# The second block's rotary embeddings: the swapped half read by VectorE from another 32-partition quadrant, in place of a permutation product on TensorE

## The chip, the cores and the metric

The kernel runs on one core of a Trainium2 chip. The metric is the device time of one execution in microseconds (us); it was measured three times before the change, and one further execution was profiled.

## What is computed

Two transformer blocks in fp32, batch 1, 256 tokens, width 2048. The first has latent and differential attention and a convolutional GEGLU feed-forward part. The second has sparse attention with compressed, selected and windowed keys (the "A" half, heads of 128) and banded attention with a sink (the "B" half, heads of 64). The change concerns the rotary embedding of the second block alone:

```python
def _rope(x):
    ang = jnp.arange(S)[:, None] * inv[None, :]
    x1, x2 = xf[..., : d // 2], xf[..., d // 2:]
    return jnp.concatenate([x1 * cos - x2 * sin, x2 * cos + x1 * sin], axis=-1)

# in second_block, after proj = h @ w_in
qa = _rope(heads of 128);  kca, ksa, kwa = _rope(heads of 128)
qb = _rope(heads of 64);   kb = _rope(heads of 64)
```

## The kernel before

Activations lie transposed: features on the 128 partitions, the 256 tokens along the free axis, one tile of 128 features by 256 tokens after another. So a head of 128 is one tile, and its halves are partitions 0 to 63 and 64 to 127. Two heads of 64 share a tile, and each has its halves in two neighbouring groups of 32 partitions.

Every fp32 weight is streamed once from HBM in halves of 128 x 1024 elements (512 KB) through a ring of eight slots, `raw`. For each half ScalarE makes a rounded copy `w_hi` (`hi`, L1138), then VectorE the remainder `w_lo` = `raw` - `w_hi` (`lo`, L1568). TensorE then takes three products for each 128 x 128 tile (L609 to L611). `w_hi` and `w_lo` are rings of four halves: half h+4 can be split once TensorE has finished half h. When `lo` of a half has run, its slot in `raw` is loaded again.

The stretch that matters is the second block's input projection, a loop over j = 0 to 46, one output tile ("unit") for each j: 16 weight tiles, two halves, 48 matmuls. Each engine has its own instruction stream with the same loop, and semaphores tie them together. In step j:

- TensorE does unit j, then for j = 31 to 38 a `compress` unit (two more halves of weights, 24 products in all, L992 to L994), then in some steps a rotation's product (`rotate`, L714), and from j = 13 on the attention work of one head.
- ScalarE splits the halves (`ahead`), and does exponentials and copies.
- VectorE does `ahead(u, 0)`, which is `lo` of the half four ahead of unit j's first; takes unit j out of PSUM into `proj2` (L2117, waits for the end of unit j); from j = 13 the softmax pieces (`first_half`); `ahead(u, 1)`; for j = 31 to 38 two more `lo`; and after all that, in twelve of the steps, a rotation (`rope2`).

A rotation takes one tile (j = 2) or two (j = 3, 5, 7, 9, 20, 24, 26, 33, 35, 37, 39). TensorE multiplies the tiles, in fp32, by a 128 x 128 matrix of 0, 1 and -1 (`swap32` for heads of 64, `swap64` for heads of 128) into PSUM; this gives the other half of each pair with its sign. VectorE then multiplies that by the sine (L1702), the tiles in place by the cosine (L1704), and adds (L1706):

```python
V.tensor_tensor(part, ps[:, bank, 0:n * S]..., sin..., ALU.mult).then_inc(rot_used, 1)
V.tensor_tensor(tiles, tiles, cos..., ALU.mult).then_inc(rope_cos, 1)
dve.wait_ge(rope_cos, at + 1)
V.tensor_tensor(tiles, tiles, part, ALU.add).then_inc(roped, 1)
dve.wait_ge(roped, at + 1)
```

`part` is the last quarter of `dk_second`. The tiles that step j rotates were taken out in steps up to j - 1, so TensorE's wait ahead of its product is for the evacuation of unit j - 1.

Of the kernel before, what the change touches and what calls it, by code (L numbers as in the profile page):

```python
# [23 lines left out]
P = 128  # L24
S = 256
# [245 lines left out]
def build_program(nc, A):  # L271
    from contextlib import ExitStack
    ctx = ExitStack()
    with ctx:
# [3 lines left out]
        def sem(name):  # L278
            return ctx.enter_context(nc.semaphore(name))
# [108 lines left out]
            sem("sub_sq"), sem("sub_mean"), sem("sub_root"), sem("sub_raw"), sem("sub_hi"), sem("sub_lo"))  # L388
        sub_ms, sub_inv, sub_wide = sem("sub_ms"), sem("sub_inv"), sem("sub_wide")
        lat_norm, lat_hi, lat_lo = sem("lat_norm"), sem("lat_hi"), sem("lat_lo")  # L390
        rope_cos = sem("rope_cos")
        conv_center, gelu_done, prod_done, g_hi_done, g_lo_done = (
            sem("conv_center"), sem("gelu_done"), sem("prod_done"), sem("g_hi_done"), sem("g_lo_done"))
        y_zero = sem("y_zero")
# [208 lines left out]
        def _(pe):  # L603
# [105 lines left out]
            def rotate(at, bank, src, tile, swap, n, used=0):  # L709

                if used:
                    pe.wait_ge(rot_used, used)
                for k in range(n):
                    last = nc.tensor.matmul(ps[:, bank, k * S:k * S + S], con(swap), src[:, tile + k, :],  # L714
                                            start=True, stop=True)
                last.then_inc(rot_ready, 1)
# [329 lines left out]
            for j in range(N_IN2):  # L1046
                tiles = range(KT) if j < N_IN2 - 1 else [*range(HEADS, KT), *range(HEADS)]
                if j >= 2:
                    unit(U2["in", j], tiles, h_hi, h_lo, middle=(lambda: compress_scores(0)) if j == 42 else None)
                before = EVAC_COUNT[U2["in", j]] - 1  # L1050
                if j == CMP_AFTER:
                    pe.wait_ge(tok_copied, 15)
                if CMP_AFTER <= j < CMP_AFTER + 8:
                    compress(j - CMP_AFTER)
                if j == 2:
                    pe.wait_ge(unit_evac, before)
                    rotate(3, 5, proj2, KB, "swap32", 1)
                elif j == 4:
                    pe.wait_ge(roped, 4)
                    nc.tensor.matmul(ps[:, OUT, 0:S], con("swap64"), proj2[:, KB, :], start=True, stop=True  # L1060
                                     ).then_inc(swap_ready, 1)
                elif j in (3, 5, 7, 9):
                    pe.wait_ge(unit_evac, before)
                    at = 4 + (j - 3) // 2
                    rotate(at, 5, proj2, QB + j - 3, "swap32", 2, at)
                elif j == 10:
                    pe.wait_ge(unit_evac, before)
                    pe.wait_ge(rot_used, 8)
                    to_tokens(12, proj2, [VB], 1)
                elif j == 20:  # L1070
                    pe.wait_ge(unit_evac, before)
                    pe.wait_ge(tok_copied, 13)
                    rotate(8, 5, proj2, KCA, "swap64", 2)
                elif j == 24:
                    pe.wait_ge(unit_evac, before)
                    rotate(9, 5, proj2, KSA, "swap64", 2, 9)
                elif j == 26:
                    pe.wait_ge(unit_evac, before)
                    rotate(10, 5, proj2, KWA, "swap64", 2, 10)
                elif j == 28:  # L1080
                    pe.wait_ge(unit_evac, before)
                    pe.wait_ge(rot_used, 11)
                    to_tokens(13, proj2, [VSA])
                elif j == 30:
                    pe.wait_ge(unit_evac, before)
                    pe.wait_ge(tok_copied, 14)
                    to_tokens(14, proj2, [VWA])
                elif j in (33, 35, 37, 39):
                    pe.wait_ge(unit_evac, before)
                    at = 11 + (j - 33) // 2  # L1090
                    rotate(at, SCORE + (at - 11) % 2, proj2, QA + j - 33, "swap64", 2, at - 1)
                elif j == 40:
                    pe.wait_ge(unit_evac, before)
                    pe.wait_ge(rot_used, 14)
                    to_tokens(15, proj2, [GA], 1)
                if j == 13:
                    pe.wait_ge(roped, 8)
                    pe.wait_ge(tok_copied, 13)
                    pe.wait_ge(swap_copied, 2)
                    pe.wait_ge(pad_ready, HEADS + 3)  # L1100
                elif j == A_STEP:
                    pe.wait_ge(roped, 15)
                    pe.wait_ge(tok_copied, 16)
                if j == 36:
                    compress_rows(0)
                elif j == 40:
                    compress_rows(1)
                elif j == 41:
                    compress_kv()
                elif j == 42:  # L1110
                    compress_scores(1)
                if B_STEP <= j < B_STEP + 19:
                    step(b_maps, j - B_STEP)
                if j == N_IN2 - 1:
                    pe.wait_ge(cmp_T_copied, 2)
                if j >= A_STEP:
                    step(a_maps, j - A_STEP)
                if j in (44, 45):
                    compress_turn(j - 44)
# [441 lines left out]
        def _(dve):  # L1561
# [134 lines left out]
            def rope(at, bank, scratch, src, tile, n, cos, sin, out=None):  # L1696

                dve.wait_ge(rot_ready, at + 1)
                part = scratch[:, 0:n * S].rearrange("p (a b) -> p a b", a=n)
                wide = [P, n, S]  # L1700
                tiles = src[:, tile:tile + n, :]
                V.tensor_tensor(part, ps[:, bank, 0:n * S].rearrange("p (a b) -> p a b", a=n),  # L1702
                                sin.unsqueeze(1).broadcast_to(wide), ALU.mult).then_inc(rot_used, 1)
                V.tensor_tensor(tiles, tiles, cos.unsqueeze(1).broadcast_to(wide), ALU.mult).then_inc(rope_cos, 1)  # L1704
                dve.wait_ge(rope_cos, at + 1)
                V.tensor_tensor(tiles if out is None else out, tiles, part, ALU.add).then_inc(roped, 1)  # L1706
                dve.wait_ge(roped, at + 1)
# [388 lines left out]
                if a < len(some):  # L2096
                    maxima(some[a])

            def rope2(at, bank, tile, d, n=2):
                rope(at, bank, rope_part.rearrange("p a b -> p (a b)"), proj2, tile, n, con(f"cos{d}"), con(f"sin{d}"))  # L2100

            def b_low():

# [6 lines left out]
            for j in range(N_IN2):  # L2110
                u = U2["in", j]
                if j == N_IN2 - 1:
                    b_low()
                if j:
                    ahead(u, 0)
                dve.wait_ge(gemm_step, unit_step(u))
                V.tensor_tensor(proj2[:, IN2_TILES[j], :], ps[:, BANK[u], 0:S], rstd[:, NORM["x2"] % 2, :], ALU.mult  # L2117
                                ).then_inc(unit_evac, 1)
                if B_STEP <= j < B_STEP + 17:
                    first_half(b_maps, j - B_STEP)  # L2120
                if j >= A_STEP:
                    first_half(a_maps, j - A_STEP)
                if j:
                    ahead(u, 1)
                if CMP_AFTER <= j < CMP_AFTER + 8:
                    for part in range(2):
                        ahead(U2["cmp", j - CMP_AFTER], part)
                if j == 2:
                    rope2(3, 5, KB, 64, 1)
                elif j in (3, 5, 7, 9):  # L2130
                    rope2(4 + (j - 3) // 2, 5, QB + j - 3, 64)
                elif j == 20:
                    rope2(8, 5, KCA, 128)
                elif j == 22:
                    dve.wait_ge(roped, 9)
                    compress_input(0, KCA, "k_pos", None)
                elif j == 24:
                    rope2(9, 5, KSA, 128)
                    split_blocks(0)
                elif j == 25:  # L2140
                    compress_input(1, VCA, "v_pos", U2["in", 21])
                elif j == 26:
                    rope2(10, 5, KWA, 128)
                elif j == 27:
                    split_blocks(1)
                elif j in (33, 35, 37, 39):
                    at = 11 + (j - 33) // 2
                    rope2(at, SCORE + (at - 11) % 2, QA + j - 33, 128)
                elif j == 42:
                    compress_shift()  # L2150
                elif j == 43:
                    compress_normalise()
                a = j - B_STEP
                if 3 <= a < len(b_maps) + 3 and b_maps[a - 3]["last"]:
                    take_b(b_maps[a - 3])
# [205 lines left out]
```

## Time and profile before

| what | value |
|---|---|
| median of 3 runs | 1762.83 us (1761.37 to 1764.17) |
| the profiled execution's own time | 1761.64 us |
| its span, first to last instruction | 1759.8 us |
| TensorE (PE) busy | 1696.8 us, 96% of the span |
| VectorE (DVE) busy | 1251.7 us, 71% |
| ScalarE (ACT) busy | 892.1 us, 51% |
| mean granted TensorE clock | 0.985 |
| DMA | 377.10 MB, mean 214 GB/s |
| load of one half of weights, issue to landing | 3.8 us |

The busy times of the engines overlap. Matmuls are pipelined in the rows: a product of the main stream shows 0.28 us, but they start every 0.12 us, so what one costs is read from the distance of starts. The input projection of the second block takes about 1285 to 1605 us of the span. A time such as 1517.36 is in us from the first instruction.

### The profile page before, as it was taken

How to read it: one execution, taken by the hardware profiler on the slowest of the kernel's cores; microseconds unless marked ns; L12 is line 12 of the kernel's file. 1: busy time of each engine (PE TensorE's matmuls, PEld its weight loads, DVE VectorE, ACT ScalarE, POOL GpSimd, SP SyncE). 2: the span in 40 equal slices, each digit the busy share in tenths (PEclk: the TensorE clock that was granted, in tenths of full speed). 3: DMA queues.
4: the chain of work that ended last, by engine and by line, in shares of the span. 5: the costliest groups of instructions: out<-in, count | busy, mean ns of one | idle time of the engine just before them, and what ended most of it. 6: DMA issues, size and time to landing. Idle time of an engine off the chain costs nothing.

```text
span 1759.8 us, 33243 instructions
## 1 busy us (share of the span) xinstructions
PE 1696.8 (96%) x13841; PEld 1654.6 (94%) x13841; DVE 1251.7 (71%) x1877; ACT 892.1 (51%) x1445; POOL 19.7 (1%) x31
## 2 busy tenths in 40 slices
PE   2899999999999999999999999999999999999997
PEld 2799999999999999999999999999899999999997
DVE  6888899898787667667667656656865576665655
ACT  8545445555565445445445435535734544446554
POOL 0000010000000000000000000000000000000000
PEclk7899999999999999999999999999999999999999
DMA  9899787688647666667667666565355444764341
GB/s 366 337 359 375 253 296 287 243 296 328 259 159 231 209 205 227 214 204 229 209 193 232 217 187 183 180 189 183 109 169 168 144 133 132 225 209 130 111 128 63
DMA packets 89285, 377.10 MB, mean 214 GB/s; under 512 B 10032, under 2 KB 10416, under 8 KB 76592
## 3 DMA queue, kind: packets, MB, share of 16 engines
q1 hardware_dynamic: 89136, 374.98, 62.7%
q8 instruction: 110, 1.80, 0.4%
q14 instruction: 39, 0.32, 0.1%
HBM read 372.84 MB, written 2.10 MB: 213 GB/s over the span
## 4 chain that ended last, share of the span: by engine, by line
PE 89%; DVE 5%; DMA 3%; issue 1%; ACT 1%; DVEq 0%; SPq 0%; ACTq 0%
PE ps L609 26%; PE ps L610 25%; PE ps L611 25%; PE ps L730 4%; DMA raw<-in_ada 3%; DVE raw L1577 2%; PE ps L764 1%; PE ps L749 1%; PE ps L772 1%; DVE w_lo L1568 1%; PE ps L714 1%; PE ps L992 0%; PE ps L994 0%; PE ps L993 0%; PE ps L638 0%
## 5 line engine op out<-in xcount | busy, mean ns | idle before, releaser
L609 PE MATMUL ps<-h_hi,w_hi 128*128 128x256 f32 x3248 | 938.4, 289 | 8.3 <-DVE h_lo L1641 5.2
L610 PE MATMUL ps<-h_lo,w_hi 128*128 128x256 f32 x3248 | 920.4, 283 | 0.0
L611 PE MATMUL ps<-h_hi,w_lo 128*128 128x256 f32 x3248 | 920.2, 283 | 0.0
L1568 DVE TENSOR_TENSOR w_lo<-raw,w_hi 128x1024 fp32r<-128x1024 f32 x510 | 622.7, 1223 | 262.7 <-ACT w_hi L1138 261.7
L1138 ACT ACTIVATE w_hi<-raw 128x1024 fp32r<-128x1024 f32 x510 | 538.6, 1058 | 511.5 <-PE ps L611 466.5
L609 PEld LDWEIGHTS ps<-h_hi,w_hi 128*128 128x128 f32 x3248 | 624.2, 192 | 16.7 <-issue 11.5
L610 PEld LDWEIGHTS ps<-h_lo,w_hi 128*128 128x128 f32 x3248 | 624.7, 192 | 1.2
L611 PEld LDWEIGHTS ps<-h_hi,w_lo 128*128 128x128 f32 x3248 | 624.4, 192 | 0.0
L1577 DVE SCALAR_TENSOR_TENSOR raw<-raw,c_wide 128x2048 f32<-128x2048 f32 x96 | 219.3, 2287 | 18.3 <-DMA raw<-in_ada 17.4
L609 PE MATMUL ps<-g_hi,w_hi 128*128 128x256 f32 x704 | 199.3, 283 | 0.6 <-DVE conv L1975 0.6
L610 PE MATMUL ps<-g_lo,w_hi 128*128 128x256 f32 x704 | 199.2, 283 | 0.0
L611 PE MATMUL ps<-g_hi,w_lo 128*128 128x256 f32 x704 | 199.2, 283 | 0.0
L609 PEld LDWEIGHTS ps<-g_hi,w_hi 128*128 128x128 f32 x704 | 135.2, 192 | 0.8 <-DVE conv L1975 0.8
L611 PEld LDWEIGHTS ps<-g_hi,w_lo 128*128 128x128 f32 x704 | 135.2, 192 | 0.0
L610 PEld LDWEIGHTS ps<-g_lo,w_hi 128*128 128x128 f32 x704 | 135.2, 192 | 0.0
L1390 ACT ACTIVATE conv<-ps,params 128x256 f32<-128x256 f32 x88 | 49.8, 565 | 148.5 <-PE ps L611 148.5
L1972 DVE SCALAR_TENSOR_TENSOR conv<-ps,params,conv 128x255 f32<-128x255 f32 x88 | 42.5, 483 | 79.4 <-ACT conv L1390 79.4
L1206 ACT ACTIVATE probs<-ps,stats 128x128 f32<-128x128 f32 (+1 forms) x112 | 48.8, 440 | 50.7 <-DVE stats L1720 43.9
L2003 DVE TENSOR_TENSOR y<-ps,y 128x256 f32<-128x256 f32 x96 | 40.4, 423 | 44.4 <-PE ps L611 44.4
L1716 DVE TENSOR_REDUCE stats<-ps 128x1 f32<-128x128 f32 (+1 forms) x112 | 37.7, 377 | 19.8 <-PE ps L733 19.6
L1975 DVE SCALAR_TENSOR_TENSOR conv<-ps,params,conv 128x255 f32<-128x255 f32 x88 | 42.5, 483 | 3.1
L1221 ACT ACTIVATE probsT<-ps 128x384 f32<-128x384 f32 (+1 forms) x56 | 29.9, 534 | 18.3 <-PE ps L749 16.9
(237 smaller groups left out, 1208.6 us busy)
## 6 DMA issues: line engine op xcount, KB each, us to landing
raw<-in_weights SPq DMA_DIRECT2D x510, 512.0 KB, 3.8
raw<-in_ada SPq DMA_DIRECT2D x96, 1024.0 KB, 6.0
x<-in_x SPq DMA_DIRECT2D x1, 2048.0 KB, 12.7
out_y<-x SPq DMA_DIRECT2D x3, 512.0 KB, 2.9
c_wide<-in_c_wide SPq DMA_DIRECT2D x1, 1024.0 KB, 5.4
consts<-in_consts SPq DMA_DIRECT2D x1, 798.0 KB, 8.9
out_y<-x SPq DMA_DIRECT2D x2, 256.0 KB, 2.6
params<-in_params SPq DMA_DIRECT2D x1, 504.0 KB, 7.4
```

What stands on the lines that cost most here:

```text
L609: nc.tensor.matmul(out, wh, hi[:, k, :], start=start, stop=False)
L610: nc.tensor.matmul(out, wh, lo[:, k, :], start=False, stop=False)
L611: last = nc.tensor.matmul(out, wl, hi[:, k, :], start=False, stop=stop)
L730: last = nc.tensor.matmul(out, q(qt), k(qt, w), start=a == 0, stop=a == n_terms - 1 and not masked)
L1138: nc.scalar.activation(w_hi[:, h % W_SLOTS, :], raw[:, raw_slot("w", h), :], ACT.Copy).then_inc(hi_split, 1)
L1206: last = nc.scalar.activation(probs[:, s, off:off + w], ps[:, SCORE + i % 2, off:off + w], ACT.Exp, bias=stats[:, s, 2 + qt:3 + qt], scale ...
L1390: nc.scalar.activation(conv[:, j, :], ps[:, BANK[u], 0:S], ACT.Identity, bias=params[:, col + b:col + b + 1], scale=params[:, col + w1:col ...
L1568: V.tensor_tensor(w_lo[:, h % W_SLOTS, :], raw[:, raw_slot("w", h), :], w_hi[:, h % W_SLOTS, :].bitcast(F32), ALU.subtract).then_inc(lo_dv ...
L1577: V.scalar_tensor_tensor(out=part, in0=part, scalar=1.0, in1=c_wide[:, :, :], op0=ALU.mult, op1=ALU.mult, accum_out=mod_raw[:, v, t:t + 1] ...
L1972: V.scalar_tensor_tensor(out=conv[:, j, 1:S], in0=ps[:, BANK[u], 0:S - 1], scalar=params[:, w0:w0 + 1], in1=conv[:, j, 1:S], op0=ALU.mult, ...
L1975: V.scalar_tensor_tensor(out=conv[:, j, 0:S - 1], in0=ps[:, BANK[u], 1:S], scalar=params[:, w2:w2 + 1], in1=conv[:, j, 0:S - 1], op0=ALU.m ...
L2003: V.tensor_tensor(y[:, f, :], ps[:, BANK[u], 0:S], y[:, f, :], ALU.add).then_inc(unit_evac, 1)
```

## The change

On TensorE the twelve `rotate` calls of the second block go, with their waits (23 fp32 products, each of a 128 x 128 matrix with 256 columns). Two waits that stood in front of them or guarded the PSUM banks move to the next user or go. On VectorE the single sine product, which read PSUM, becomes four `scalar_tensor_tensor` instructions of 32 partitions each: each reads a group of 32 partitions of the tiles and the same group of the sine table, multiplies by 1 or -1, and writes another group of `part`. For heads of 64 groups 0 and 1, and 2 and 3, change places; for heads of 128 groups 0 and 2, and 1 and 3. The cosine product now waits for all four. The first block's rotations and the one `swap64` product at j = 4 stay on TensorE.

```diff
-                if j == 2:
-                    pe.wait_ge(unit_evac, before)
-                    rotate(3, 5, proj2, KB, "swap32", 1)
-                elif j == 4:
+                if j == 4:
...
-                elif j in (3, 5, 7, 9):
-                    pe.wait_ge(unit_evac, before)
-                    at = 4 + (j - 3) // 2
-                    rotate(at, 5, proj2, QB + j - 3, "swap32", 2, at)
                 elif j == 10:
                     pe.wait_ge(unit_evac, before)
-                    pe.wait_ge(rot_used, 8)
                     to_tokens(12, proj2, [VB], 1)
-                elif j == 20:
+                elif j == 28:
                     pe.wait_ge(unit_evac, before)
                     pe.wait_ge(tok_copied, 13)
-                    rotate(8, 5, proj2, KCA, "swap64", 2)
...
-                elif j in (33, 35, 37, 39):
-                    pe.wait_ge(unit_evac, before)
-                    at = 11 + (j - 33) // 2
-                    rotate(at, SCORE + (at - 11) % 2, proj2, QA + j - 33, "swap64", 2, at - 1)
...
-            def rope2(at, bank, tile, d, n=2):
-                rope(at, bank, rope_part.rearrange("p a b -> p (a b)"), proj2, tile, n, con(f"cos{d}"), con(f"sin{d}"))
+            def rope2(at, u, tile, d, n=2):
+
+                part, shape = rope_part[:, 0:n, :], [32, n, S]
+                tiles = proj2[:, tile:tile + n, :]
+                dve.wait_ge(unit_evac, EVAC_COUNT[u] - 1)
+                for q in range(4):
+                    away = (1 if d == 64 else 2)
+                    src = q ^ away
+                    rows = slice(32 * src, 32 * src + 32)
+                    V.scalar_tensor_tensor(out=part[32 * q:32 * q + 32], in0=tiles[rows], scalar=-1.0 if q < src else 1.0,
+                                           in1=con(f"sin{d}")[rows].unsqueeze(1).broadcast_to(shape),
+                                           op0=ALU.mult, op1=ALU.mult).then_inc(rope_sine, 1)
+                dve.wait_ge(rope_sine, 4 * (at - 2))
+                V.tensor_tensor(tiles, tiles, con(f"cos{d}").unsqueeze(1).broadcast_to([P, n, S]), ALU.mult
+                                ).then_inc(rope_cos, 1)
+                dve.wait_ge(rope_cos, at + 1)
+                V.tensor_tensor(tiles, tiles, part, ALU.add).then_inc(roped, 1)
+                dve.wait_ge(roped, at + 1)
```

What this does to VectorE's stream is seen in step 33, the first rotation of the query heads of 128 (`proj` is `proj2`, `consts` holds the tables). Before, with what each instruction waits for:

```order
L2117 TENSOR_TENSOR proj<-ps,rstd 128x256 [waits gemm_step]
L1568 TENSOR_TENSOR w_lo<-raw,w_hi 128x1024 [waits hi_split] x3
L1702 TENSOR_TENSOR dk_second<-ps,consts 128x512 [waits rot_ready]
L1704 TENSOR_TENSOR proj<-proj,consts 128x512
L1706 TENSOR_TENSOR proj<-proj,dk_second 128x512 [waits rope_cos]
L1568 TENSOR_TENSOR w_lo<-raw,w_hi 128x1024 [waits hi_split,roped]
```

And now:

```order
L2110 TENSOR_TENSOR proj<-ps,rstd 128x256 [waits gemm_step]
L1545 TENSOR_TENSOR w_lo<-raw,w_hi 128x1024 [waits hi_split] x3
L2085 SCALAR_TENSOR_TENSOR dk_second<-proj,consts 32x512 [waits unit_evac]
L2085 SCALAR_TENSOR_TENSOR dk_second<-proj,consts 32x512 x3
L2089 TENSOR_TENSOR proj<-proj,consts 128x512 [waits rope_sine]
L2092 TENSOR_TENSOR proj<-proj,dk_second 128x512 [waits rope_cos]
L1545 TENSOR_TENSOR w_lo<-raw,w_hi 128x1024 [waits hi_split,roped]
```

Three instructions more stand between the `lo` ahead of the rotation and the `lo` behind it, and the cosine product has a wait that it had not.

On TensorE, at the end of step 33 (the last product of `compress`, the rotation, the first product of unit 34), before:

```order
L994 MATMUL ps<-w_hi,cmp_xl 30x256
L714 MATMUL ps<-proj,consts 128x256 [waits rot_used,unit_evac]
L714 MATMUL ps<-proj,consts 128x256
L609 MATMUL ps<-h_hi,w_hi 128x256 [waits lo_dve,unit_evac]
L610 MATMUL ps<-h_lo,w_hi 128x256
```

And now:

```order
L994 MATMUL ps<-w_hi,cmp_xl 30x256
L609 MATMUL ps<-h_hi,w_hi 128x256 [waits lo_dve,unit_evac]
L610 MATMUL ps<-h_lo,w_hi 128x256
```

The two fp32 products and their wait are gone; unit 34's first product still waits for its `lo` and for its PSUM bank.

## Rows read from the trace of the kernel before

**Rows 1.** Busy time by stretch: us, then PE, PEld, DVE, ACT, POOL, clock, DMA.

```profile
1285.00:1605.00 320.00, 320.00 (x2568) 305.65 (x2567) 200.02 (x324) 150.68 (x224) 1.01 (x3) 1.00 0.54 168
1500.00:1580.00 80.00, 80.00 (x657) 77.32 (x656) 52.65 (x56) 37.15 (x40) 0.00 (x0) 1.00 0.72 225
1605.00:1755.00 150.00, 144.89 (x1132) 135.16 (x1131) 92.36 (x218) 80.33 (x165) 0.00 (x0) 0.99 0.30 96
```

**Rows 2.** Who waited for whom, 1285 to 1605: us, times, longest.

```profile
ACT w_hi L1138 <- PE ps L611: 153.4, 80, 3.6
DVE w_lo L1568 <- ACT w_hi L1138: 94.6, 77, 4.0
DVE proj L2117 <- PE ps L611: 20.0, 38, 2.3
PEld ps L609 <- issue: 3.0, 17, 0.2
```

**Rows 3.** The rotations' products, 1285 to 1600, grouped by line and form.

```profile
L714 PE MATMUL ps<-proj,consts 128*128 128x256 f32 x46 | 11.9, 379 | 0.0
```

**Rows 4.** TensorE in order of time at steps 2 and 33: start, us.

```profile
1287.29 0.28 PE L611 MATMUL ps<-h_hi,w_lo 128*128 128x256 f32 x1
1287.41 0.59 PE L714 MATMUL ps<-proj,consts 128*128 128x256 f32 x2
...
1287.96 0.28 PE L610 MATMUL ps<-h_lo,w_hi 128*128 128x256 f32 x1
...
1517.24 0.28 PE L994 MATMUL ps<-w_hi,cmp_xl 128*30 128x256 f32 x1
1517.36 1.02 PE L714 MATMUL ps<-proj,consts 128*128 128x256 f32 x4
...
1518.34 0.28 PE L610 MATMUL ps<-h_lo,w_hi 128*128 128x256 f32 x1
```

**Rows 5.** The chain that ended last: first and last of eleven such lines.

```profile
1293.75 0.86 PE ps L714 x4
...
1569.29 0.86 PE ps L714 x4
```

**Rows 6.** VectorE in order of time at step 33, with idle time before.

```profile
1518.71 1.23 DVE L1568 TENSOR_TENSOR w_lo<-raw,w_hi 128x1024 fp32r<-128x1024 f32 x1 [0.15 <-ACT w_hi L1138]
1519.85 0.68 DVE L1702 TENSOR_TENSOR dk_second<-ps,consts 128x512 f32<-128x512 f32 x1
1520.45 0.68 DVE L1704 TENSOR_TENSOR proj<-proj,consts 128x512 f32<-128x512 f32 x1
1521.17 0.69 DVE L1706 TENSOR_TENSOR proj<-proj,dk_second 128x512 f32<-128x512 f32 x1
1522.52 1.23 DVE L1568 TENSOR_TENSOR w_lo<-raw,w_hi 128x1024 fp32r<-128x1024 f32 x1 [0.66 <-ACT w_hi L1138]
```

**Rows 7.** `scalar_tensor_tensor` forms of VectorE: count, us, mean ns, idle.

```profile
L1827 DVE SCALAR_TENSOR_TENSOR cs<-cs 128x256 f32<-128x256 f32 x3 | 1.3, 425 | 0.1
L1927 DVE SCALAR_TENSOR_TENSOR proj<-proj,lam,ps 128x512 f32<-128x512 f32 x4 | 2.7, 740 | 0.0
```

**Rows 8.** Line L1811, four copies of groups 0 to 3: durations, then in order of time.

```profile
L1811 DVE COPY delta<-delta_parts x4: 152/156/160, 9.5 to 10.0; 32x24 bf16<-32x24 bf16 x4
...
9.50 0.66 DVE L1811 COPY delta<-delta_parts 32x24 bf16<-32x24 bf16 x4
```

**Rows 9.** The ScalarE split ahead of that last `lo`, and the weight load that needs it.

```profile
1521.36 1.06 ACT L1138 ACTIVATE w_hi<-raw 128x1024 fp32r<-128x1024 f32 x1 [2.68 <-PE ps L611]
...
1526.66 0.19 PEld L609 LDWEIGHTS ps<-h_hi,w_hi 128*128 128x128 f32 x1
```

**Rows 10.** VectorE in order of time, steps 24 and 25.

```profile
1443.91 0.68 DVE L1702 TENSOR_TENSOR dk_second<-ps,consts 128x512 f32<-128x512 f32 x1
...
1445.96 1.16 DVE L2055 TENSOR_TENSOR cmp_xl<-dk_second,cmp_xh 128x960 fp32r<-128x960 f32 x1
1447.33 1.23 DVE L1568 TENSOR_TENSOR w_lo<-raw,w_hi 128x1024 fp32r<-128x1024 f32 x1 [0.22 <-ACT w_hi L1138]
1449.06 0.42 DVE L2117 TENSOR_TENSOR proj<-ps,rstd 128x256 f32<-128x256 f32 x1 [0.51 <-PE ps L611]
...
1457.02 0.42 DVE L2117 TENSOR_TENSOR proj<-ps,rstd 128x256 f32<-128x256 f32 x1 [0.50 <-PE ps L611]
```

**Rows 11.** TensorE's four transposed-row products at step 36, in the chain.

```profile
1544.83 0.56 PE ps L1002 x4
```

More of the change, by code:

```diff
@@ L390, in build_program @@
         lat_norm, lat_hi, lat_lo = sem("lat_norm"), sem("lat_hi"), sem("lat_lo")
-        rope_cos = sem("rope_cos")
+        rope_cos, rope_sine = sem("rope_cos"), sem("rope_sine")
         conv_center, gelu_done, prod_done, g_hi_done, g_lo_done = (
@@ L1061, in _ @@
                                      ).then_inc(swap_ready, 1)
-                elif j in (3, 5, 7, 9):
-                    pe.wait_ge(unit_evac, before)
-                    at = 4 + (j - 3) // 2
-                    rotate(at, 5, proj2, QB + j - 3, "swap32", 2, at)
                 elif j == 10:
                     pe.wait_ge(unit_evac, before)
-                    pe.wait_ge(rot_used, 8)
                     to_tokens(12, proj2, [VB], 1)
-                elif j == 20:
+                elif j == 28:
                     pe.wait_ge(unit_evac, before)
                     pe.wait_ge(tok_copied, 13)
-                    rotate(8, 5, proj2, KCA, "swap64", 2)
-                elif j == 24:
-                    pe.wait_ge(unit_evac, before)
[L1076 to L1082, printed above, removed]
                     to_tokens(13, proj2, [VSA])
@@ L1087, in _ @@
                     to_tokens(14, proj2, [VWA])
-                elif j in (33, 35, 37, 39):
-                    pe.wait_ge(unit_evac, before)
-                    at = 11 + (j - 33) // 2
-                    rotate(at, SCORE + (at - 11) % 2, proj2, QA + j - 33, "swap64", 2, at - 1)
                 elif j == 40:
                     pe.wait_ge(unit_evac, before)
-                    pe.wait_ge(rot_used, 14)
                     to_tokens(15, proj2, [GA], 1)
@@ L2128, in _ @@
                 if j == 2:
-                    rope2(3, 5, KB, 64, 1)
+                    rope2(3, u, KB, 64, 1)
                 elif j in (3, 5, 7, 9):
-                    rope2(4 + (j - 3) // 2, 5, QB + j - 3, 64)
+                    rope2(4 + (j - 3) // 2, u, QB + j - 3, 64)
                 elif j == 20:
-                    rope2(8, 5, KCA, 128)
+                    rope2(8, u, KCA, 128)
                 elif j == 22:
@@ L2137, in _ @@
                 elif j == 24:
-                    rope2(9, 5, KSA, 128)
+                    rope2(9, u, KSA, 128)
                     split_blocks(0)
@@ L2142, in _ @@
                 elif j == 26:
-                    rope2(10, 5, KWA, 128)
+                    rope2(10, u, KWA, 128)
                 elif j == 27:
@@ L2147, in _ @@
                     at = 11 + (j - 33) // 2
-                    rope2(at, SCORE + (at - 11) % 2, QA + j - 33, 128)
+                    rope2(at, u, QA + j - 33, 128)
                 elif j == 42:
```

## The prediction

> **What bounds the kernel now.** I read the busy time by stretch first. In the input projection of the second block TensorE is busy for 320.00 of 320.00 us, at the full granted clock of 1.00, which is the 2.4 GHz level; VectorE is busy for 200.02 and ScalarE for 150.68 us, and the DMA engines for 0.54 of it [rows 1]. After it, up to 1755 us, TensorE is still busy for 144.89 of 150 us. Next the list of waits for the same 320 us: the other two engines wait for TensorE (ScalarE 153.4 us before a split, VectorE 20.0 us before it takes out a unit, and 94.6 us for ScalarE, which itself waits for TensorE). The longest entry of the weight loads is "issue", 3.0 us over 17 times, and no line names a DMA [rows 2]. So this stretch is as long as TensorE's work, and everything behind it starts relative to TensorE. Work taken off TensorE comes off the end, as long as `w_lo` stays ahead of it.
>
> **What goes from TensorE.** The page counts 46 records of the rotation's product, two for each of 23 fp32 products [rows 3]. Their shown length (379 ns) overlaps, so I take the distance of starts. In step 2, one product: L611 starts at 1287.29, and without a rotation the next L610 would start two pitches of 0.12 us later, at 1287.53; it starts at 1287.96 [rows 4]. One product costs 0.43 us. In step 33, two products: L994 starts at 1517.24, the second product of the next unit would start at 1517.48, and starts at 1518.34 [rows 4]: 0.86 us. The chain that ended last names the two-product rotation eleven times with the same 0.86 us [rows 5]. Sum: 11 x 0.86 + 0.43 = 9.9 us, all on the path. The semaphore waits that go with them cost nothing: no idle time of TensorE stands before them [rows 2]. For the same reason the two waits that are kept and moved (steps 28 and 10) are taken at nothing; what they wait for was done a step before.
>
> **What comes to VectorE.** Now a rotation starts at 1519.85, the next two instructions at 1520.45 and 1521.17, and the last ends at 1521.86 [rows 6]. An instruction that waits for nothing starts 0.60 us after one of 512 elements; one that waits for its predecessor's semaphore, 0.72 us after it. The new four have 32 partitions and 512 elements each. No row here has that form, so I bound it. The time of a VectorE instruction goes by the elements of a partition: 512 take 0.683 and 1024 take 1.23 us [rows 6], which gives about 0.41 us at 256; the `scalar_tensor_tensor` of 256 elements with a constant took 0.425 us, one of 512 with a scalar from memory and PSUM took 0.740 [rows 7]. I take 0.695 for the new ones, between 0.68 and 0.74. Partitions bring no discount: four copies of 32 partitions with 24 elements took 0.152 to 0.160 us each [rows 8], and nothing in those rows looks like a quarter.
>
> Next the distance. Those four copies, each on another group of 32 partitions, took 0.66 us together, (0.66 - 0.156) / 3 = 0.168 us apart, so none began before the one in front had ended [rows 8]; the 0.60 us between instructions of 0.68 that stay on all partitions [rows 6] is an overlap. The new four change their group each time, so I take 0.71 us apart and 0.1 us lost before the first. The Trainium skill (VectorE: DVE Perf Modes, section "Two Vector instructions with no wait between them") gives this as a rule: an instruction whose input or output starts in another 32-partition quadrant than the last one's is held until all earlier ones have finished. By the rule the four stand a full duration apart, without it 0.60; the sum for the kernel is the same 9.9 us by either, if the margin below holds.
>
> A rotation of two tiles then runs: first of four at 1519.95, last at 1522.08, cosine at 1522.80, sum at 1523.52, and the `lo` behind it can start at 1524.24. Before, that `lo` could have started at 1521.90 for VectorE, and did at 1522.52, when ScalarE had finished its half. VectorE gets 2.3 us more in each of eleven steps and some 1.4 in step 2, about 27 us. It had 120 us idle in the stretch [rows 1], so its sum of work is covered; the question is how late one `lo` may be.
>
> **Where the cover is thinnest.** The tightest steps are those in which `compress` follows the next unit, since its halves are used up in 1.4 us each: 33, 35 and 37. The `lo` behind the rotation of step 33 is the first half of unit 35, which TensorE's weight load took up at 1526.66 [rows 9]. With the rotation's 0.86 us gone TensorE gets there at 1525.80. The `lo` now ends at 1524.24 + 1.23 = 1525.47, and with 0.1 us for the signal (a split that ended at 1522.42 let VectorE start at 1522.52, [rows 6, 9]) TensorE may go on at 1525.57: 0.23 us to spare, where before it had 2.8. With the four 0.60 us apart the margin is 0.66 us; with 0.75 us apart (the 0.740 row) it is 0.07. Step 37 has the same order of work. Step 35 has 0.56 us more, since four small products stand in TensorE's way to unit 37 [rows 11]. I cost all three at nothing. If the four are dearer, each 0.1 us more costs up to 0.4 us in each of them, once: behind it come four `lo` with room to catch up.
>
> Elsewhere the room is wide. In step 24, where the rotation is followed by a 1.16 us split of the compressed input [rows 10], VectorE gets to its next `lo` at about 1449.4 instead of 1447.33 and to the evacuation of unit 25 some 2.3 us late. That `lo` is for unit 27, wanted behind unit 26, which ends just before 1457.02 [rows 10]: over 5 us to spare. The softmax pieces behind it run a step ahead of the transposes that need them. In steps 3 to 9 and 39 there is no `compress` behind, and a `lo` has three halves of 2.9 us (24 products, 0.12 us apart). VectorE's lateness also delays loads, since `lo` frees the slot: by at most 2.4 us in a ring of eight halves, with DMA at 0.72 in the densest part [rows 1] and no wait for it [rows 2].
>
> **Sum.** 1761.64 (the profiled execution) - 9.9 + 0 = 1751.7 us. The median of the three runs is 1.2 us above that execution, so I say 1762.83 - 9.9 = 1752.9 us.
>
> **Rivals.**
> 1. *Part of it comes back as waits for `w_lo` in steps 33, 35 and 37.* For: the margin of 0.23 us rests on a price for which there is no row. With the four 1.0 us apart the loss is 4 x 0.29 - 0.23 = 0.93 us in steps 33 and 37 and 0.37 in step 35, together 2.2 us: 1755.1 us. Against: the nearest rows lie at 0.60 to 0.75.
> 2. *No change that can be told.* The four cost twice the nearest row, 1.42 us apart: 12 x 0.71 - 1.25 = 7.3 us lost in the three steps, 1760.2 us. For: reading one group and writing another in the same instruction is not in the trace (the copies of [rows 8] kept their group). Against: those copies show no such cost for a change of group from one to the next.
> 3. *Slower.* VectorE runs such an instruction at a quarter of the rate, about 2.8 us each. In the same three steps 12 x 2.13 - 1.25 = 24.3 us of waiting for `w_lo` against 9.9 saved: 1777.2 us. The point of no gain is 12 x (p - 0.71) - 1.25 = 9.9, p = 1.64 us apart; slower by 0.2% begins at 1.93 us, 2.7 times the nearest row. Nothing in the profile speaks for it but the absence of a row.
>
> On the second and third only a page has a statement: the Trainium skill (Vector Engine (DVE) Microarchitecture Reference, section 3.8) says that a 32-partition operation may write to any quadrant at no cost. No row here shows it.
>
> **How the numbers follow.** 0.2% of this kernel is 3.5 us, about what a measurement can tell from no change. The full saving I give 0.86, the partial one 0.08 (between 3.5 and 9 us saved), no change 0.03, slower 0.03. So faster has 0.94, same 0.03, slower 0.03. The three runs lay within 1.5 us of their median, which puts the full saving at 1751.4 to 1754.4; the range reaches a little below, for a fast set of runs, and above to 1756.5, to take in most of the first rival: 1750.5 to 1756.5.
>
> **What will show it.** In the changed profile the 46 records of the rotation's product are gone from this stretch, and VectorE's evacuations of units 33 and 34 stand 0.86 us closer than before. The four 32-partition instructions read 0.68 to 0.74 us, and their group of four 2.8 to 2.9 us. TensorE has no wait on `w_lo` in steps 33 to 39. A wait there of more than 0.1 us would show the margin too small; a wait of TensorE in steps 20 to 28 would show that I misread the room of the softmax pieces; and a total saving below 9 us without a wait on TensorE would mean that the 0.86 us was not all the products' own. The prediction goes wrong if the new form costs over 0.9 us, or if a cost of one instruction on TensorE hides in the pitch of the main stream.

## The result and the profile after

The changed kernel takes 1753.05 us (median of 4 runs, 1751.56 to 1754.85), against 1762.1 us (4 runs, 1761.04 to 1764.17) for the one before. The ratio is 0.9946, with a 95% interval of 0.9933 to 0.9959; that is 7 to 12 us less. 1752.9 us was forecast. The profiled execution has a span of 1749.7 us, 10.1 us under that of before, and the median lies 9.05 us under.

The busy times by stretch of the changed kernel, in the columns of [rows 1] (the first row is the input projection of the second block, 10 us shorter than before; the last is the work behind it):

```profile
1285.00:1595.00 310.00, 310.00 (x2521) 296.84 (x2520) 223.06 (x360) 150.21 (x225) 1.34 (x3) 1.00 0.55 174
1500.00:1570.00 70.00, 70.00 (x587) 67.97 (x586) 56.60 (x63) 35.20 (x38) 0.00 (x0) 1.00 0.70 229
1595.00:1745.00 150.00, 144.74 (x1131) 135.02 (x1129) 92.42 (x218) 80.24 (x165) 0.00 (x0) 0.99 0.31 96
```

TensorE is still busy without a gap, at the full clock; VectorE is busy for 23 us more in 10 us less time and fills 81% of the densest part, where it filled 66%. The work behind the stretch is as it was.

The list of waits of the changed kernel, 1285 to 1600 us:

```profile
ACT w_hi L1115 <- PE ps L611: 143.2, 80, 3.6
DVE w_lo L1545 <- ACT w_hi L1115: 66.4, 51, 4.0
DVE proj L2110 <- PE ps L611: 14.4, 25, 2.3
...
PEld ps L609 <- issue: 3.2, 18, 0.2
```

VectorE's own idle time has shrunk (94.6 to 66.4 us before `lo`, 20.0 to 14.4 before an evacuation, [rows 2]); TensorE's has not grown (the eighteenth entry of L609, 0.2 us, stands at 1597.44 in the stretch behind; with the window drawn out to 1611 the kernel before has 18 too).

Step 33, VectorE in order of time, which answers to [rows 6] (a merged row names how many instructions it holds):

```profile
1511.99 1.23 DVE L1545 TENSOR_TENSOR w_lo<-raw,w_hi 128x1024 fp32r<-128x1024 f32 x1 [0.16 <-ACT w_hi L1115]
1513.25 2.83 DVE L2085 SCALAR_TENSOR_TENSOR dk_second<-proj,consts 32x512 f32<-32x512 f32 x4
1516.11 0.69 DVE L2089 TENSOR_TENSOR proj<-proj,consts 128x512 f32<-128x512 f32 x1
1516.84 0.69 DVE L2092 TENSOR_TENSOR proj<-proj,dk_second 128x512 f32<-128x512 f32 x1
1517.56 1.22 DVE L1545 TENSOR_TENSOR w_lo<-raw,w_hi 128x1024 fp32r<-128x1024 f32 x1
```

And the weight load that waits for this last `lo`, as in [rows 9]:

```profile
1519.08 0.19 PEld L609 LDWEIGHTS ps<-h_hi,w_hi 128*128 128x128 f32 x1
```

From the start of the `lo` in front to the start of the `lo` behind it is 5.57 us, against 5.53 forecast. That `lo` ends at 1518.78; with 0.1 us for the signal 0.2 us are to spare.

### The profile page after: what moved, and what is told of

It reads as the page before. It is cut to its first block, busy times and chain, and to the rows that moved or that the text cites. A ratio compares the mean times of both kernels' runs of the same rounds, so it can differ in the third digit from the quotient of the medians.

```text
span 1749.7 us, 33174 instructions
## 1 busy us (share of the span) xinstructions
PE 1688.6 (97%) x13795; PEld 1646.9 (94%) x13795; DVE 1275.7 (73%) x1913; ACT 891.1 (51%) x1445; POOL 20.0 (1%) x31
## 4 chain that ended last, share of the span: by engine, by line
PE 88%; DVE 5%; DMA 4%; issue 1%; ACT 1%; SPq 0%; DVEq 0%; ACTq 0%
PE ps L609 26%; PE ps L610 25%; PE ps L611 25%; PE ps L730 4%; DMA raw<-in_ada 4%; DVE raw L1554 2%; PE ps L764 2%; PE ps L749 1%; PE ps L772 1%; DVE w_lo L1545 1%; PE ps L992 0%; PE ps L993 0%; PE ps L994 0%; PE ps L638 0%; PE ps L652 0%
## 5 line engine op out<-in xcount | busy, mean ns | idle before, releaser
L609 PE MATMUL ps<-h_hi,w_hi 128*128 128x256 f32 x3248 | 936.5, 288 | 6.7 <-DVE h_lo L1618 4.4
L611 PE MATMUL ps<-h_hi,w_lo 128*128 128x256 f32 x3248 | 919.9, 283 | 0.0
L609 PEld LDWEIGHTS ps<-h_hi,w_hi 128*128 128x128 f32 x3248 | 624.0, 192 | 15.3 <-issue 9.8
L611 PEld LDWEIGHTS ps<-h_hi,w_lo 128*128 128x128 f32 x3248 | 624.1, 192 | 0.0
L609 PE MATMUL ps<-g_hi,w_hi 128*128 128x256 f32 x704 | 199.3, 283 | 0.6 <-DVE conv L1952 0.6
L611 PE MATMUL ps<-g_hi,w_lo 128*128 128x256 f32 x704 | 199.2, 283 | 0.0
L609 PEld LDWEIGHTS ps<-g_hi,w_hi 128*128 128x128 f32 x704 | 135.2, 192 | 0.8 <-DVE conv L1952 0.8
L611 PEld LDWEIGHTS ps<-g_hi,w_lo 128*128 128x128 f32 x704 | 135.2, 192 | 0.0
## 6 DMA issues: line engine op xcount, KB each, us to landing
x<-in_x SPq DMA_DIRECT2D x1, 2048.0 KB, 12.7
```

Of the source, the lines that this page charges most:

```text
L609: nc.tensor.matmul(out, wh, hi[:, k, :], start=start, stop=False)
L611: last = nc.tensor.matmul(out, wl, hi[:, k, :], start=False, stop=stop)
```

## The experiments

The first four ran on one chip, the next four on a second and key_copies on a third, with the kernel before beside them at 1761.7, 1761.1 and 1761.8 us. A median of four runs is good to about 1 us, so effects under that are read in the traces.

**products_kept: is it the products?**

```diff
+                if j in ROTATIONS:
+                    n, bank = ROTATIONS[j]
+                    for k in range(n):
+                        nc.tensor.matmul(ps[:, bank, k * S:k * S + S], con("swap64"), con("cos128"),
+                                         start=True, stop=True)
```

> The changed kernel, but TensorE still makes its 23 fp32 products in the same steps, of the permutation matrix with the cosine table, into the same PSUM banks; nobody reads them and VectorE does not wait for them. Theory A (the saving is what the products cost on TensorE, 0.43 us one and 0.86 us two): all of it goes back, 9.9 us above the changed kernel, 1763 us. Theory C (the saving came from VectorE no longer waiting for TensorE, or from PSUM banks that come free earlier): the time stays near 1753 us.

1763.1 us, ratio to the kernel before 1.0009 (1.0000 to 1.0019). The whole saving is gone with the new VectorE code in place, so the saving is what the products cost. The waits and the PSUM banks that came free are worth nothing that can be measured; the median lies 1.4 us above that of the kernel before, at the edge of what the runs tell. The products that were kept look in the trace as the old ones did ([rows 3]):

```profile
L1080 PE MATMUL ps<-consts 128*128 128x256 f32 x46 | 11.9, 378 | 0.0
```

**no_swap_at_all: did VectorE's new work take a part?**

```diff
-                for q in range(4):
...
+                V.tensor_tensor(part, tiles, con(f"sin{d}").unsqueeze(1).broadcast_to([P, n, S]), ALU.mult
+                                ).then_inc(rope_sine, 4)
```

> The changed kernel with one sine product of 128 partitions in place of the four of 32; it multiplies each half by its own sine and not by the other half's, so the rotation is not computed; VectorE's work is as before the change, and TensorE has no products. Theory A: VectorE's 27 us lie under TensorE, so the time is that of the changed kernel, 1753 us within 1 us. Theory B (part of the saving was lost again to VectorE's new work): faster than the changed kernel by what was lost, 1 us or more.

1751.45 us, ratio 0.9947 (0.9933 to 0.9962), against 0.9946 for the change; its span is 1749.6 us against 1749.7. VectorE's added work costs nothing that can be measured, and the waits of the weight loads in this stretch are the same in both traces.

**one_more: how thin is the cover?**

```diff
-                for q in range(4):
+                for at_q, q in enumerate([0, 1, 2, 3, 0]):
...
+                    to = part if at_q < 4 else gated[:, 0:n, :]
```

> The changed kernel with a fifth 32-partition instruction in each rotation, into a buffer that nobody reads. It makes the rotation 0.71 us longer. In the changed kernel's trace the lo behind step 33's rotation ends at 1518.78 and the weight load that needs it starts at 1519.08; with 0.1 us for the signal 0.2 us are to spare. Theory A (thin margin): a wait of TensorE of 0.5 us in step 34 and another in step 38, none in step 36, where 0.56 us more stand in between, and none elsewhere: 1754 us. Theory B (the margin is wide): no wait and the changed kernel's time.

1751.87 us, ratio 0.9951 (0.9936 to 0.9965): the 1 us is below what the runs tell. The trace tells it. These are the two weight loads that find their `lo` late, with the idle time in front; in the changed kernel there is none at these places:

```profile
1518.94 0.19 PEld L609 LDWEIGHTS ps<-h_hi,w_hi 128*128 128x128 f32 x1 [0.55 <-issue]
1554.34 0.19 PEld L609 LDWEIGHTS ps<-h_hi,w_hi 128*128 128x128 f32 x1 [0.55 <-issue]
```

Behind the rotations of steps 33 and 37, and not behind that of step 35, as expected. 0.71 us more gave 0.55 us of waiting: the margin was about 0.16 us.

**twice: where does VectorE begin to bound?**

```diff
+                for at_q, q in enumerate([0, 1, 2, 3, 0, 1, 2, 3]):
```

> The changed kernel with each of the four 32-partition instructions made twice, the second time into a buffer that nobody reads: 2.84 us more in each rotation of two tiles. Theory A (thin margin): waits of TensorE of 2.6 us after the rotations of steps 33 and 37 and of 2.1 us after that of step 35, 7.3 us together, 1760.4 us; no wait after the other rotations, though VectorE has the same work more there. Theory B (wide margin): the changed kernel's time. If VectorE were the bound by its sum of work, 12 times 2.8 us would come on top: 1787 us.

1767.2 us, ratio 1.0036 (1.0023 to 1.0049): slower than before the change, and twice the loss that was expected. The weight loads that waited, by place:

```profile
1306.03 0.19 PEld L609 LDWEIGHTS ps<-h_hi,w_hi 128*128 128x128 f32 x1 [0.80 <-issue]
1318.53 0.19 PEld L609 LDWEIGHTS ps<-h_hi,w_hi 128*128 128x128 f32 x1 [0.94 <-issue]
1331.04 0.19 PEld L609 LDWEIGHTS ps<-h_hi,w_hi 128*128 128x128 f32 x1 [0.95 <-issue]
1343.54 0.19 PEld L609 LDWEIGHTS ps<-h_hi,w_hi 128*128 128x128 f32 x1 [0.71 <-issue]
...
1457.38 0.19 PEld L764 LDWEIGHTS ps<-probsT,proj 128*64 128x64 f32 x2 [1.23 <-issue]
1474.55 0.19 PEld L764 LDWEIGHTS ps<-probsT,proj 128*64 128x64 f32 x2 [1.00 <-issue]
...
1527.72 0.19 PEld L609 LDWEIGHTS ps<-h_hi,w_hi 128*128 128x128 f32 x1 [2.69 <-issue]
1547.45 0.19 PEld L609 LDWEIGHTS ps<-h_hi,w_hi 128*128 128x128 f32 x1 [1.99 <-issue]
1567.23 0.29 PEld L609 LDWEIGHTS ps<-h_hi,w_hi 128*128 128x128 f32 x1 [2.70 <-issue]
```

The last three are the 7.3 us that were expected (2.69 + 1.99 + 2.70 = 7.4). Two groups were not. In steps 3 to 9 the first four rows stand 12.5 us apart: a rotation comes every second step, and two steps of VectorE then hold four `lo`, two evacuations and a rotation of 7.2 us, more than TensorE's two units of 5.75 us. Each `lo` there had room, but the sum over two steps had not; that makes 3.4 us. Behind the rotations of steps 24 and 26 a product of the attention (L764) waited for a PSUM bank that VectorE empties at the end of its step (L1754), which makes 1.9 us beyond the usual 0.17. The waits sum to 12.7 us, where the profiled span is 15.2 us above that of the changed kernel. A part of the rest is the clock. The stretch with the last wait and the one behind it:

```profile
1565.00:1570.00 5.00, 2.74 (x13) 2.77 (x14) 4.93 (x7) 0.96 (x1) 0.00 (x0) 0.72 0.33 107
1570.00:1575.00 5.00, 5.00 (x41) 5.00 (x41) 2.31 (x3) 1.23 (x2) 0.00 (x0) 0.94 0.88 291
```

The granted clock fell to a mean of 0.72 and 0.94 and was back at 1.00 after that. Cut into single microseconds, it is 1.00 up to 1567, 0.50 (the 1.2 GHz level) from 1568 to 1570, when TensorE is busy again, and 1.00 from 1571. I estimate the loss at 5 x 0.28 + 5 x 0.06 = 1.7 us. The last 0.8 us are not traced.

**one_group and own_group: what sets the distance of the four?**

```diff
-                    src = q ^ away
+                    src = 0
+                    to = (part, gated[:, 0:n, :], proj2[:, ZA + 4:ZA + 4 + n, :], proj2[:, ZA + 6:ZA + 6 + n, :])[q]
...
+                    V.scalar_tensor_tensor(out=to[0:32], in0=tiles[rows], ...
```

That is one_group. In own_group the edit is `src = q` alone, with the output as in the change.

> The changed kernel, but all four 32-partition instructions read partitions 0 to 31 and write partitions 0 to 31 of four different buffers, so none changes its group; the rotation is not computed. If a change of group is what holds each of the four until the one in front has ended, they stand 0.60 us apart here (4 of them in 2.5 us) instead of 0.71 (2.8 us). If the distance comes with 32 partitions or with this operation, it stays 2.8 us. The total stays that of the changed kernel, 1753 us.

> The changed kernel, but each of the four reads and writes its own group of partitions (0, 1, 2, 3), so the group changes from one to the next but never between input and output; the rotation is not computed. If the change from one instruction to the next holds them, 2.8 us for the four; if it is the crossing within an instruction, 2.5 us. Duration of one 0.68 us in either case if crossing is free, less than that if crossing costs. Total 1753 us.

Step 33 of one_group:

```profile
1514.32 0.67 DVE L2086 SCALAR_TENSOR_TENSOR dk_second<-proj,consts 32x512 f32<-32x512 f32 x1
1514.92 0.67 DVE L2086 SCALAR_TENSOR_TENSOR gated<-proj,consts 32x512 f32<-32x512 f32 x1
1515.52 1.28 DVE L2086 SCALAR_TENSOR_TENSOR proj<-proj,consts 32x512 f32<-32x512 f32 x2
```

And of own_group:

```profile
1516.54 2.82 DVE L2085 SCALAR_TENSOR_TENSOR dk_second<-proj,consts 32x512 f32<-32x512 f32 x4
```

One group: 0.60 us apart, 2.48 us for the four. Own group, without any crossing: 2.82 us, as in the change with its crossing (2.83). So the 0.11 us comes with the change of group from one instruction to the next, and reading one group and writing another costs nothing. One_group also writes to four buffers where own_group writes to one. That this is not what lets its instructions overlap is seen in a row of the kernel before, four `scalar_tensor_tensor` of 0.740 us into one tile, all on the same partitions:

```profile
336.37 2.71 DVE L1927 SCALAR_TENSOR_TENSOR proj<-proj,lam,ps 128x512 f32<-128x512 f32 x4
```

They stand (2.71 - 0.740) / 3 = 0.66 us apart, less than one of them takes. As for crossing, the median duration is 0.682 us without and 0.684 us with it. The single times, 1753.3 and 1755.3 us, say nothing against the expectation of 1753.

**halves_of_64: fewer instructions.**

```diff
+                size = d // 2
+                for q in range(P // size):
+                    src = q ^ 1
...
+                    V.scalar_tensor_tensor(out=part[size * q:size * q + size], in0=tiles[rows], ...
```

> The changed kernel, with two instructions of 64 partitions in place of four of 32 for the heads of 128. The rotation of two tiles is 1.4 us shorter on VectorE in steps 20 to 39. Theory A: TensorE did not wait in those steps, so the time stays within 1 us of the changed kernel's, 1753 us, and the margin behind step 33's rotation grows from 0.2 to 1.6 us. Theory B (some of the saving is lost to VectorE's work): faster by 1 us or more. An instruction of 64 partitions takes 0.68 us like one of 32.

1753.19 us, ratio 0.9951 (0.9938 to 0.9965), and two instructions of 64 partitions take 1.40 us, half of 2.83:

```profile
1513.36 1.40 DVE L2085 SCALAR_TENSOR_TENSOR dk_second<-proj,consts 64x512 f32<-64x512 f32 x2
...
1516.24 1.22 DVE L1545 TENSOR_TENSOR w_lo<-raw,w_hi 128x1024 fp32r<-128x1024 f32 x1
```

1.4 us of VectorE's time in each of seven rotations is given back and the kernel is no faster: that time was not on the path. The `lo` of the second row ends at 1517.46 and the weight load that needs it starts at 1519.18, so the margin is 1.6 us, as expected.

**all_on_vector and key_copies: can the other products go too?**

```diff
-                    rotate(0, 5, proj1, KR, "swap32", 1)
...
-                    rotate(1, 5, uq, QR, "swap32", 2, 1)
...
-                    rotate(2, 5, uq, QR + 2, "swap32", 2, 2)
...
-                    nc.tensor.matmul(ps[:, OUT, 0:S], con("swap64"), proj2[:, KB, :], ...
+                    V.tensor_copy(proj2[0:64, KB + 1, :], proj2[64:128, KB, :]).then_inc(swap_copied, 1)
+                    V.tensor_copy(kb_second[64:128, 0, :], proj2[0:64, KB, :]).then_inc(swap_copied, 1)
```

all_on_vector has the whole of it, with four instructions of 32 partitions in the first block's `rope` as well; key_copies only the last three lines. Both stand on halves_of_64. With the product of the keys go the two copies by which ScalarE took it out of PSUM.

> The kernel before it, with the first block's three rotations (five fp32 products) and the second block's swap64 product of the keys (one) done on VectorE too. Theory A: where TensorE is busy without a gap the six products are worth 0.43 us each, 2.6 us in all: 1750.4 us. A rival for the first block: VectorE is busy there for 0.8 to 0.9 of the time, so the 1.4 to 2.3 us that each rotation now takes more make w_lo late, and the saving of 2.15 us there is lost or turns into a loss of up to 3 us; then 1753 to 1756 us.

1760.8 us, ratio 0.9992 (0.9984 to 1.0001), no longer to be told from the kernel before: this edit loses 7.6 us against halves_of_64 by the medians. Key_copies below keeps its gain with the keys' part alone, so the loss is the first block's. In that block VectorE also runs the modulation products of 2.3 us (L1577 before) and stands on the path. Its two rotations of `uq` came before the split that TensorE needs for the first unit of the output projection; this is the second of them:

```profile
345.55 2.83 DVE L1663 SCALAR_TENSOR_TENSOR gated<-uq,cs 32x512 f32<-32x512 f32 x4
348.41 0.69 DVE L1667 TENSOR_TENSOR uq<-uq,cs 128x512 f32<-128x512 f32 x1
349.13 0.69 DVE L1669 TENSOR_TENSOR uq<-uq,gated 128x512 f32<-128x512 f32 x1
349.91 2.36 DVE L1899 TENSOR_TENSOR h_lo<-proj,h_hi 128x1024 fp32r<-128x1024 f32 x2
...
351.25 0.29 PEld L609 LDWEIGHTS ps<-h_hi,w_hi 128*128 128x128 f32 x1 [4.24 <-issue]
```

The split (L1899) starts at 349.91, and in the changed kernel at 344.28. TensorE waits 4.24 us, the stretch 350 to 360, in which the wait ends, has a mean granted clock of 0.66, and by 362 us VectorE's stream is 8.0 us behind that of the changed kernel (362.43 against 354.44 at the first maxima of the next attention). The forecast loss of up to 3 us was too small. By the last weight loads of L672, in front of the second block (1271.3 against 1260.0), it is 11.3 us; the last 3.3 us I did not trace.

> The kernel with two instructions of 64 partitions for the heads of 128, and with the swap64 product of the keys in step 4 (one fp32 product) replaced by two copies of 64 partitions on VectorE; the first block's rotations stay on TensorE. Theory A: the product goes for 0.43 us and the copies are hidden, so 0.4 us under the kernel with two instructions of 64 partitions, 1752.6 us by the medians so far, too little for the medians to tell; in the trace VectorE's evacuations of units 4 and 5 stand 5.75 us apart instead of 6.18, and no wait on w_lo appears. The rival from all_on_vector, that the second block's part also lost there, would show as a wait of TensorE between 1290 and 1320 us.

1752.8 us (6 runs), ratio 0.9947 (0.9933 to 0.9961), no wait of TensorE in the stretch. The 0.4 us cannot be told from none in the times. In the trace of TensorE's own starts it is there: halves_of_64 has 0.66 us from the last L611 ahead of the keys' product to the second product behind it, key_copies 0.24 at that place. The marker that was named for it failed: VectorE's evacuations of units 4 and 5 were to stand 5.75 us apart in place of 6.18, and they stand 3.65 apart (1301.98 and 1305.63), since the one of unit 4 comes late, behind the rotation of step 3; in halves_of_64 it is 3.99 already. So no version beats the change by a measurable amount; what is left of these products is worth less than the noise (the keys) or stands where VectorE has no time to spare (the first block).

## Why the prediction was right

**The bound.** Right. In this stretch TensorE had no idle time before and has none after, and what was taken off it came off the end: 10.1 us by the two profiled spans, 9.05 us by the medians. That the forecast of 1752.9 us lies only 0.15 us from the median is luck, since a median of four runs is good to about 1 us.

**The products, 9.9 us.** Right: shown by products_kept, which stands 10.05 us above the changed kernel by the medians and 9.4 by the profiled spans. The distance of starts was the right price. The 379 ns of a row would have given another sum: 46 x 0.379 = 17 us if added up, 11.9 us by the busy time of [rows 3].

**VectorE's price, 0.695 us each and 0.71 apart.** Measured 0.684 and 0.71 ((2.83 - 0.684) / 3 = 0.715). From its first instruction to the `lo` behind it a rotation of two tiles takes 4.31 us (1513.25 to 1517.56) in place of 2.05, 2.26 more against 2.3 forecast. The rule of the Trainium skill (VectorE: DVE Perf Modes, section "Two Vector instructions with no wait between them") that an instruction which starts in another quadrant (group of 32 partitions) is held agrees: 0.60 us apart with one quadrant, 0.71 with changing ones. The statement of the Trainium skill (Vector Engine (DVE) Microarchitecture Reference, section 3.8) that a 32-partition operation crosses quadrants for free agrees too: 0.682 and 0.684 us.

**The margin of 0.23 us in steps 33 and 37.** Right: 0.2 us in the trace, about 0.16 by one_more; so the first rival failed by that little. The prices that the prediction itself allowed, 0.60 to 0.75 us apart, gave margins from 0.66 to 0.07.

**"Elsewhere the room is wide".** Right for this change and too generous as a statement. For a single `lo` it holds (unit 25 is taken out at 1445.00, 1.8 us late, without effect: TensorE starts what follows the unit at 1443.00, and before the change unit 25 was taken out 0.2 us after that start), but I did not add up VectorE's work over the two steps of a cycle in steps 3 to 9, nor the bank that the attention product waits for. The slack of the cycle was 11.5 - (12.5 - 2.86) = 1.9 us per rotation. So the second rival was priced wrongly: at twice the price the kernel is not 7.3 but 14 us above the changed one, which is slower than before, and the point of no gain lies below 1.42 us apart, not at 1.64. The forecast does not rest on it, as the price was right.

**A marker that was wrong.** I wrote that the evacuations of units 33 and 34 would stand 0.86 us closer. They stand 10.65 us apart, where they had stood 9.40 (1514.77 and 1524.17), since the second comes behind the longer rotation:

```profile
1508.05 0.42 DVE L2110 TENSOR_TENSOR proj<-ps,rstd 128x256 f32<-128x256 f32 x1 [0.50 <-PE ps L611]
1518.70 0.42 DVE L2110 TENSOR_TENSOR proj<-ps,rstd 128x256 f32<-128x256 f32 x1
1525.14 0.43 DVE L2110 TENSOR_TENSOR proj<-ps,rstd 128x256 f32<-128x256 f32 x1 [0.50 <-PE ps L611]
```

The second row has no idle time in front: VectorE was late, it did not wait for TensorE. Over two units, when VectorE has caught up, it is 1508.05 to 1525.14, 17.09 us, against 17.95 before: the 0.86 us. The same kind of marker was chosen again for key_copies and failed again. To date TensorE's work, its own starts should be named, not those of an engine that may be late.

## What to carry to other kernels

Price an instruction of a pipelined engine by the distance of starts with and without it, and find the one consumer for which the added work of the other engine comes latest; here that is a weight load 9.3 us behind the old product, with 0.2 us to spare. Then add up the engine's work over a whole cycle of the loop as well, since both limits can bind in different steps. The same kind of edit gained about 9 us by the medians where VectorE was busy for 63% of the time, and lost 7.6 us in a place where VectorE itself was on the path.

## What the runs showed of the hardware

A short wait of TensorE can cost more than itself. In all_on_vector TensorE waited 4.24 us, up to 351.25; the granted clock fell while it still waited (0.61 from 350 to 351), was 0.50, the 1.2 GHz level, from 351 to 357, and 1.00 again from 358. In twice the third of three waits of 2.0 to 2.7 us was followed by a fall to 0.50, while the two before it left the clock at 1.00 in the stretches of 5 us around them. What decides that, the runs do not show. An instruction of 64 partitions that reads one half and writes the other takes as long as one of 32 (0.687 and 0.683 us, halves_of_64).

One more: GpSimd's copy of 64 partitions by 256 elements (of the keys, behind the `swap64` product of step 4) took 0.40 us in the kernel before and in no_swap_at_all, where VectorE was idle beside it. It took 0.73 us in the changed kernel, 1.13 in products_kept and 1.45 in key_copies, each time beside VectorE instructions with two inputs from SBUF. In one_group the copy started 0.05 us ahead of such an instruction, a `lo`; the copy took 0.40 us and the `lo` 1.43 in place of 1.23. This suggests that the later of the two is held up by the earlier one; nothing waited for the copy, and no run was made to settle the cause.
